# A two-layer Hyena and RWKV-7 step on one core: SyncE's load queue of the RWKV scan in another order

## The chip, the cores and the metric

The kernel runs on one core of one Trainium2 chip. The metric is the device time of one execution of the whole program in microseconds (us), lower is better. PE is TensorE (matmuls and transposes), DVE is VectorE, ACT is ScalarE, POOL is GpSimd, and SP is SyncE, which here does nothing but request DMA transfers in the order in which its instructions stand.

## The reference, cut to what matters

640 tokens (512 latent tokens and 128 context tokens, 1024 wide) pass a Hyena layer and then a bidirectional RWKV-7 layer with 32 heads of 64. All is float32. The change touches only the recurrence of the second layer, which is run forward and backward for each head:

```python
def _wkv7_scan(r, w, k, v, a, b, s0, reverse):
    """RWKV-7 state recurrence S_t = S_{t-1}(diag(w_t) + a_t^T b_t) + v_t^T k_t ; y_t = S_t r_t.
    r,w,k,v,a,b: (B, T, H, N) float32; s0 (B, H, N, N) [value, key]."""
    def step(S, inp):
        r_t, w_t, k_t, v_t, a_t, b_t = inp
        sa = jnp.einsum("bhvk,bhk->bhv", S, a_t)
        S = S * w_t[:, :, None, :] + sa[..., :, None] * b_t[..., None, :] + v_t[..., :, None] * k_t[..., None, :]
        return S, jnp.einsum("bhvk,bhk->bhv", S, r_t)
...
    decay = jnp.exp(-jnp.exp(-jax.nn.softplus(-w_raw) - 0.5))
...
    o_f, s_f = _wkv7_scan(r_h, decay_h[0], k_dir[0], v_h, -kk, kk * iclr_h[0], s0_f, False)
    o_b, s_b = _wkv7_scan(r_h, decay_h[1], k_dir[1], v_h, -kk, kk * iclr_h[1], s0_b, True)
```

w (decay) and the learning rate iclr come from two small low-rank weights for each direction, kk is the key scaled and normalised by head. Returned are the outputs of both token groups and the final states of the context.

## The kernel before, in words

The program is a sequence of stages, each a block in which the five engines run their own instruction lists and meet only by semaphores: modulation vectors, filter, Hyena input, convolution, Hyena output, RWKV projections (`rwkv_in`, which leave keys and receptances in `scratch_rk_d` and values and gates in `scratch_vz_d`), the scan (`rwkv_scan`, L1358), and the output stage. The change is in the scan.

The scan takes 16 rounds, one for each pair of heads (128 of the 2048 inner channels). The 640 tokens stand as 10 chunks of 64. A round has two parts:

- a chunk part: PE forms the products of the scaled keys (`e_decays` with `e_bk`, the "scores"), turns the keys (into `BKT`) and the matrix `C_` (into `CT`), and then inverts a triangular 64x64 system for every chunk in five levels. A level is: transposes of `e_F` (T), the products Y (`M` with `CTm`), which ACT copies into `BDY`, the products Z (`BDY` with `M2T`), which DVE adds into `e_F`. Between them PE fills in scores left over (L1601).
- a state part of eight steps, in which the states go through the chunks (`BDS` with `e_ar`, `BDW` with `e_Q`, `UV` with `BKT`) and the outputs are summed from `BDV`, `BDU`, `BDS`. Its last output product bears the mark "O" (L1752).

While round i runs, the engines also prepare round i+1 ("prep"), in pieces put between the main work by hand: ACT squares and scales the new keys `e_k` (`e_kk`, L1771 to L1773, behind a wait for the keys' load) between the copies of `CT` and the first copy of `BDY`; PE applies the small weights `e_w` and `e_a` in levels 4 and 5; DVE builds `e_decays`, its last product of the prep bears the mark "ar"; PE transposes the start states `st` behind "O" (mark "S0", L1570). The pieces stand in each engine's one list, so a piece that waits holds up the main work that stands behind it. ACT's copies of `BDY` stand behind `e_kk`.

SP requests the loads of a round in three groups. `load_keys(j)` (L1459): keys `e_k` (128x640), the small weights `e_w` and `e_a`, receptances `e_r`, and the two start states, six transfers, behind a wait for "S0" of round j-1. `load_values(j)` (L1471): 14 transfers of the values into `BDV` and `UV`; PE waits for them at L1706, where the state part begins. `copy_ar(j)` (L1483): a copy of `e_decays` into `e_ar`, 1280 KB inside the on-chip memory, behind a wait for "ar" of round j; PE waits for it at L1707. `BDV`, `UV` and `e_ar` have one buffer each, which round i reads until its "O". POOL builds the masks `CTm`, and stores states and outputs (`Osb`) of a round behind its end; it goes on to the next round only when those stores have landed (L1524).

`Steps.now(label, i)` is the semaphore value at which the step with that label is done in round i; `Steps.before(label, i)` is the value at which it was done in round i-1 (for round 0 it holds from the start). `rounds` runs the first 15 rounds in a loop with `has_prep` true, the 16th behind it with `has_prep` false; PE's list is unrolled.

Of the kernel before, what the change touches and what calls it, by code (L numbers as in the profile page):

```python
# [1357 lines left out]
def rwkv_scan(nc, A, G, M):  # L1358
# [37 lines left out]
    with ExitStack() as st:  # L1396
# [29 lines left out]
        main, prep = kinds("main", ("pe", "act", "dve", "pool")), kinds("prep", ("pe", "act", "dve"))  # L1426
# [8 lines left out]
        def rounds(eng, kind, body):  # L1435
            steps = [s[kind] for s in (main, prep) if kind in s]
            with eng.Fori(0, KE - 1) as i:
                for s in steps:
                    s.n = 0
                body(i, True)  # L1440
            for s in steps:
                s.n = 0
            body(KE - 1, False)
# [10 lines left out]
        with nc.Block() as block:  # L1454
            @block.sync
            def _(sp):
                sp.wait_ge(s_z, 6)

                def load_keys(j):  # L1459
                    ch = bass.ds(j * P, P)  # L1460

                    sp.wait_ge(prep["pe"].sem, prep["pe"].before("S0", j))
                    sp.dma_start(k[:, :], A["rk_d"][1, ch, :]).then_inc(s_l["k"], 16)
                    for n, src, dst in (("w2", "rw_w2", lw2), ("a2", "rw_a2", la2)):
                        sp.dma_start(dst[:, :], A[src][0].rearrange("z r e -> (z r) e")[:, ch]).then_inc(s_l[n], 16)
                    sp.dma_start(r[:, :], A["rk_d"][0, ch, :]).then_inc(s_l["r"], 16)
                    for d, n in enumerate(("state_rwkv_fwd", "state_rwkv_bwd")):
                        src = A[n][0, 0].rearrange("h v k -> v h k")[:, bass.ds(2 * j, 2), :]
                        sp.dma_start(st0[HALVES[d], :].rearrange("v (h k) -> v h k", h=2), src).then_inc(s_l["st"], 16)

                def load_values(j):  # L1471
                    v_t = A["vz_d"][0].rearrange("(c t) n -> t c n", t=C)
                    for h in range(2):
                        sp.dma_start(BDV[HALVES[h], :, HALVES[h]], v_t[:, :, bass.ds(j * P + 64 * h, 64)]).then_inc(s_l["v"], 16)
                    ch = bass.ds(j * P, P)
                    sp.dma_start(UV[HIGH, 0:NS:3, :], v_t[:, 0:CS, ch]).then_inc(s_l["v"], 16)
                    sp.dma_start(UV[HIGH, 5:9:3, :], v_t[:, CS:NC, ch]).then_inc(s_l["v"], 16)
                    for n in range(CS):
                        sp.dma_start(UV[HIGH, 3 * n + 1, :], A["vz_d"][0, (CS - 1 - n) * C:(CS - n) * C, ch]).then_inc(s_l["v"], 16)
                    for n, c in ((3, NC - 1), (4, NC - 2)):  # L1480
                        sp.dma_start(UV[HIGH, 3 * n + 2, :], A["vz_d"][0, c * C:(c + 1) * C, ch]).then_inc(s_l["v"], 16)

                def copy_ar(j):  # L1483
                    sp.wait_ge(prep["dve"].sem, prep["dve"].now("ar", j))
                    sp.dma_start(ar[:, :, :, :], decays[:, :, :, :]).then_inc(s_ar, 16)

                def body(i, has_prep):
                    if has_prep:
                        load_keys(i + 1)
                        sp.wait_ge(main["pe"].sem, main["pe"].now("O", i))  # L1490
                        load_values(i + 1)
                        copy_ar(i + 1)
                load_keys(0)
                load_values(0)
                copy_ar(0)
                rounds(sp, "pe", body)

            @block.gpsimd
# [32 lines left out]
            def _(pe):  # L1531
# [41 lines left out]
                def body(i, has_prep):  # L1573
# [117 lines left out]
                    def o_terms(now, most):  # L1691
                        while terms and terms[0][0] <= now and most:
                            _, c, a, b = terms.pop(0)
                            at_ = left.pop(0)
                            out = ps[HALVES[c % 2], c // 8, c % 8 // 2 * P:(c % 8 // 2 + 1) * P]
                            last = mm(out, a, b, at_ not in opened, at_ not in left)
                            opened.add(at_)
                            most -= 1
                        if not terms:
                            return last  # L1700
# [440 lines left out]
```

## Time and profile before

| | |
|---|---|
| runs shown: median of 2 | 3990.89 us (3990.87 to 3990.91) |
| the profiled execution, its own time | 3992.75 us |
| span of the profiled execution, first to last instruction | 3990.7 us |
| busy: PE / PE weight loads / DVE / ACT / POOL | 85% / 52% / 43% / 23% / 6% of the span |
| mean granted TensorE clock | 0.911 |
| DMA, mean | 69 GB/s |
| the scan's rounds 1 to 14, as SP's value requests stand (2318.55 to 3701.08 us) | 1382.5 us |

The page gives busy shares over the whole span; the stages have different limits, so the scan is read by its own stretch. In the rows further down, a time at a row's start is us from the start of the span. In a timeline the second number is the us that the row covers, `x20` the number of instructions in it, and the bracket at the end the idle time of that engine just before, with what ended it. A `PEclk` of 1.00 is TensorE's full clock (2.4 GHz), 0.50 half of it (1.2 GHz). `L104`, `L115` and `L118` are helpers, so tile names tell the place.

### The profile page before, as it was taken

The page shows a single profiled execution, that of the slowest core. Times are in us where ns is not written, and L with a number is a line of the kernel's source. Part 1 is how long each engine was busy: PE and PEld are TensorE (multiplying, and loading weights), DVE is VectorE, ACT ScalarE, POOL GpSimd, SP SyncE. Part 2 cuts the span into 40 slices and gives each one's busy share as a digit, 9 for nine tenths or more (in the row PEclk, how much of TensorE's full clock was granted, in tenths as well). Part 3 has the DMA queues.
Part 4 walks back from the last instruction along what each step waited for, and adds up shares of the span by engine and source line. Part 5 has one row for each costly group of instructions (what it writes and reads, how often), then busy time and mean ns, then how long its engine had stood idle before and what let it go on. Part 6 is the DMA issues. An engine that isn't in the chain of part 4 may idle for free. (4 is left out here: it accounts for less than half of the span.)

```text
span 3990.7 us, 50708 instructions
## 1 busy us (share of the span) xinstructions
PE 3373.1 (85%) x18946; PEld 2066.4 (52%) x18946; DVE 1728.8 (43%) x3104; ACT 914.6 (23%) x1968; POOL 257.2 (6%) x346
## 2 busy tenths in 40 slices
PE   7599999898898685999997788888887888888759
PEld 1255555434434342555443566666666666666624
DVE  0222222266676413100001655555555555555467
ACT  0222222100000011000000333433333433333311
POOL 0000000000000000000001011111111111111100
PEclk9799999798898897999999788998889899998979
DMA  6222222311120230323221111111111111111162
GB/s 251 69 89 88 88 84 84 117 32 48 37 71 26 85 123 22 98 89 125 80 103 61 33 37 36 37 36 37 36 37 36 37 36 37 36 36 37 32 242 85
DMA packets 223386, 276.66 MB, mean 69 GB/s; under 512 B 41412, under 2 KB 168916, under 8 KB 218757
## 3 DMA queue, kind: packets, MB, share of 16 engines
q1 hardware_dynamic: 208760, 223.59, 17.8%
q0 software_dynamic: 14480, 50.87, 3.3%
q8 instruction: 124, 2.03, 0.2%
q14 instruction: 22, 0.17, 0.0%
HBM read 199.94 MB, written 53.49 MB: 64 GB/s over the span
## 5 line engine op out<-in xcount | busy, mean ns | idle before, releaser
L104 PE MATMUL ps<-hT,hw 128*128 128x512 f32 (+1 forms) x2048 | 562.2, 435 | 6.5 <-DMA hw<-in_hy_w_in 6.5
L104 PEld LDWEIGHTS ps<-hT,hw 128*128 128x128 f32 x2048 | 313.0, 192 | 253.1 <-issue 253.1
L104 PE MATMUL ps<-mix,rw 128*128 128x512 f32 (+1 forms) x1024 | 283.1, 440 | 10.9 <-DMA rw<-in_rw_w_k 5.7
L104 PE MATMUL ps<-rwv,mix 128*128 128x512 f32 x640 | 274.9, 592 | 0.8 <-ACT rout L118 0.8
L104 PE MATMUL ps<-BDS,e_ar 128*64 128x128 f32 x1152 | 176.2, 293 | 80.5 <-DVE BDS L115 40.4
L104 PEld LDWEIGHTS ps<-mix,rw 128*128 128x128 f32 x1024 | 157.3, 194 | 136.7 <-issue 136.7
L104 PEld LDWEIGHTS ps<-rwv,mix 128*128 128x128 f32 x640 | 121.5, 190 | 153.6 <-issue 152.6
L118 ACT ACTIVATE BDY<-ps 64x384 f32<-64x384 f32 (+1 forms) x320 | 138.2, 432 | 269.9 <-PE ps L104 263.6
L104 PE MATMUL ps<-BDV,AK 128*64 128x128 f32 x1280 | 184.8, 307 | 0.0
L104 PE MATMUL ps<-e_decays,e_bk 64*64 64x128 f32 x2560 | 184.4, 295 | 0.0
L104 PE MATMUL ps<-BDY,M2T 128*64 128x128 f32 x1600 | 120.3, 303 | 73.3 <-ACT BDY L118 70.3
L115 DVE TENSOR_TENSOR BDS<-ps,e_pcd 64x128 f32<-64x128 f32 x224 | 64.6, 288 | 240.4 <-PE ps L104 236.9
L118 ACT ACT_TABLE_LOAD x70 | 89.8, 1283 | 344.4 <-PE ps L104 237.1
L104 PEld LDWEIGHTS ps<-e_decays,e_bk 64*64 64x64 f32 x2560 | 153.3, 145 | 23.5 <-issue 21.7
L104 PEld LDWEIGHTS ps<-BDS,e_ar 128*64 128x64 f32 x1152 | 108.2, 140 | 108.7 <-DVE BDS L115 44.9
L1514 POOL TENSOR_TENSOR CTm<-CT,tab 128x384 f32<-128x384 f32 (+1 forms) x160 | 134.6, 862 | 444.7 <-PE ps L104 285.6
L107 DVE SCALAR_TENSOR_TENSOR mix<-xx,col,hT 128x640 f32<-128x640 f32 x48 | 38.6, 879 | 287.5 <-PE ps L104 287.5
L112 DVE TENSOR_SCALAR hcv<-hpad,hpc 128x641 f32<-128x641 f32 x48 | 29.6, 616 | 306.8 <-ACT hpad L118 306.8
L118 ACT ACTIVATE osave<-ps 128x512 f32<-128x512 f32 x64 | 38.2, 597 | 534.1 <-PE ps L104 517.1
L115 DVE TENSOR_TENSOR M<-e_F,tab 64x384 f32<-64x384 f32 (+1 forms) x320 | 155.6, 486 | 9.9
L104 PE MATMUL ps<-hsd,dft 128*128 128x512 f32 x288 | 140.8, 652 | 17.0 <-DVE hsd L115 17.0
L1646 PE MATMUL ps<-tab,e_F 128*128 128x128 f32 x400 | 80.4, 316 | 88.1 <-DVE e_F L115 53.4
(229 smaller groups left out, 5140.0 us busy)
## 6 DMA issues: line engine op xcount, KB each, us to landing
hw<-in_hy_w_in SPq DMA_DIRECT2D x64, 512.0 KB, 4.1
aw<-in_ada_w SPq DMA_DIRECT2D x16, 1536.0 KB, 6.8
e_ar<-e_decays SPq DMA_DIRECT2D x16, 1280.0 KB, 6.7
scratch_vx_d<-hot POOLq DMA_DIRECT2D x32, 320.0 KB, 2.8
scratch_rk_d<-rout POOLq DMA_DIRECT2D x32, 320.0 KB, 3.5
scratch_vz_d<-rtok POOLq DMA_DIRECT2D x40, 256.0 KB, 2.3
rw<-in_rw_w_r SPq DMA_DIRECT2D x16, 512.0 KB, 4.0
rw<-in_rw_w_k SPq DMA_DIRECT2D x16, 512.0 KB, 4.0
```

Of the source, the lines that this page charges most:

```text
L104: return nc.tensor.matmul(out, lhsT, rhs, start=first, stop=last)
L107: return nc.vector.scalar_tensor_tensor(out=out, in0=in0, scalar=scalar, in1=in1, op0=op0, op1=op1)
L112: return nc.vector.tensor_scalar(out, in0, s1, s2, op0, op1)
L115: return nc.vector.tensor_tensor(out, a, b, op)
L118: return nc.scalar.activation(out, in_, f, **kw)
L1514: main["pool"].did(nc.gpsimd.tensor_tensor(CTm[:, lv % 2, cs, :], CT[:, cs, :], m, MUL), ("CTm", lv, g))
L1646: last = nc.tensor.transpose(ps[:, T_BANK[g], (p - q.start) * P:(p - q.start + 1) * P], F[:, 2 * p:2 * p + 2, :], ident)
```

## The change

The values of a round are requested in that round itself and no more in the round before: the prologue has no `load_values(0)`; each round requests first the keys, small weights and states of the next round, then its own values (behind a wait for "O" of the round before), and then waits for its own "O" and requests the copy into `e_ar` for the next round. No transfer is added, removed or resized, and the other engines' lists stay as they are.

```diff
                 def body(i, has_prep):
                     if has_prep:
                         load_keys(i + 1)
+
+                    sp.wait_ge(main["pe"].sem, main["pe"].before("O", i))
+                    load_values(i)
+                    if has_prep:
                         sp.wait_ge(main["pe"].sem, main["pe"].now("O", i))
-                        load_values(i + 1)
                         copy_ar(i + 1)
                 load_keys(0)
-                load_values(0)
                 copy_ar(0)
                 rounds(sp, "pe", body)
```

In SP's list at the start of the scan (before its loop) the rows stand as follows; `BDV` and `UV` are the values, `e_ar` the copy, `scan_prep_dve` the semaphore of DVE's preparation.

```order
 L1469 DMA st<-in_state_rwkv_fwd 64x2x64
 L1469 DMA st<-in_state_rwkv_bwd 64x2x64
-L1474 DMA BDV<-scratch_vz_d 64x10x64 x2
-L1476 DMA UV<-scratch_vz_d 64x8x128
-L1477 DMA UV<-scratch_vz_d 64x2x128
-L1479 DMA UV<-scratch_vz_d 64x128 x8
-L1481 DMA UV<-scratch_vz_d 64x128 x2
 L1485 DMA e_ar<-e_decays 128x2560 [waits scan_prep_dve]
 L1437 UNCONDITIONAL_BRANCH
```

The 14 value transfers of round 0 are gone from here, and the copy follows the states directly.

At the end of the loop's body and behind the loop; `scan_main_pe` is the semaphore of PE's main work, on which "O" is counted, and the branch closes the loop, whose first rows are the keys.

```order
 L1481 ISA
 L1481 DMA UV<-scratch_vz_d 64x128 x2
-L1484 ISA
+L1494 REGISTER_ALU
+L1484 ISA [waits scan_main_pe]
 L1485 DMA e_ar<-e_decays 128x2560 [waits scan_prep_dve]
 L1437 REGISTER_ALU
 L1437 COMPARE_AND_BRANCH
+L1474 DMA BDV<-scratch_vz_d 64x10x64 [waits scan_main_pe]
+L1474 DMA BDV<-scratch_vz_d 64x10x64
+L1476 DMA UV<-scratch_vz_d 64x8x128
```

The wait for "O" of the present round has moved from ahead of the values to between the values and the copy, so that only the copy and, over the branch, the next keys stand right behind it; the values of the last round now stand behind the loop.

## Rows read from the trace of the kernel before

**Rows 1.** Stretches: us, busy PE, PEld, DVE, ACT, POOL, clock, DMA; rounds 1, 3.
```profile
2318.55:2417.55 99.00, 81.92 (x798) 65.54 (x798) 58.38 (x123) 39.05 (x92) 10.61 (x13) 0.90 0.13 37
...
2516.62:2613.52 96.90, 78.38 (x798) 62.53 (x798) 58.38 (x123) 39.06 (x92) 10.59 (x13) 0.93 0.14 38
```

**Rows 2.** Waits of rounds 1 to 14: us in total, times, longest.
```profile
ACT e_kk L118 <- DMA e_k<-scratch_rk_d: 102.8, 14, 8.8
...
PE ps L104 <- ACT BDY L118: 68.8, 14, 7.3
```

**Rows 3.** Timeline of PE and ACT over round 1.
```profile
2318.44 0.33 PE L1570 MATMUL ps<-tab,st 128*128 128x128 f32 x1
2325.90 1.31 PE L104 MATMUL ps<-tab,C_ 128*64 128x128 f32 x20 [0.20 <-ACT BKT L118]
2331.23 2.40 PE L104 MATMUL ps<-M,CTm 128*64 128x128 f32 x20
2336.42 1.55 ACT L118 ACTIVATE e_kk<-e_k,e_pc 128x640 f32<-128x640 f32 x2 [7.04 <-DMA e_k<-scratch_rk_d]
2339.13 2.40 PE L104 MATMUL ps<-BDY,M2T 128*64 128x128 f32 x20 [4.17 <-ACT BDY L118]
2371.06 0.65 PE L104 MATMUL ps<-BDV,AK 128*64 128x128 f32 x4
2417.44 0.33 PE L1570 MATMUL ps<-tab,st 128*128 128x128 f32 x1
```

**Rows 4.** Timeline of SP's queue at the start of round 1, and of round 15.
```profile
2318.55 1.39 SPq L1474 DMA_DIRECT2D BDV<-scratch_vz_d  x2
...
2326.86 1.77 SPq L1481 DMA_DIRECT2D UV<-scratch_vz_d  x2
2328.77 0.51 SPq L1485 DMA_DIRECT2D e_ar<-e_decays  x1
2329.86 0.34 SPq L1463 DMA_DIRECT2D e_k<-scratch_rk_d  x1
...
2335.06 0.61 SPq L1469 DMA_DIRECT2D st<-in_state_rwkv_bwd  x1
...
3701.08 1.39 SPq L1474 DMA_DIRECT2D BDV<-scratch_vz_d  x2
```

**Rows 5.** Timeline of SP, PE and ACT at the start of round 0.
```profile
2225.82 0.35 SPq L1463 DMA_DIRECT2D e_k<-scratch_rk_d  x1
2234.03 1.31 PE L104 MATMUL ps<-tab,C_ 128*64 128x128 f32 x20 [0.20 <-ACT BKT L118]
2238.53 1.55 ACT L118 ACTIVATE e_kk<-e_k,e_pc 128x640 f32<-128x640 f32 x2 [1.02 <-DVE e_pc L1875]
2243.03 1.31 PE L104 MATMUL ps<-BDY,M2T 128*64 128x128 f32 x20
```

**Rows 6.** Granted clock by stretch: round 1 behind the wait, round 0 at its masks.
```profile
2338.50:2341.00 2.50, 1.87 (x18) 1.90 (x20) 0.28 (x1) 1.24 (x3) 0.00 (x0) 0.50 0.00 0
...
2239.50:2242.00 2.50, 2.50 (x24) 2.04 (x22) 0.69 (x1) 1.33 (x3) 1.20 (x2) 0.50 0.03 7
2242.00:2244.50 2.50, 2.34 (x38) 1.92 (x36) 1.24 (x2) 0.97 (x3) 0.95 (x2) 0.98 0.00 0
```

**Rows 7.** From request to landing: the keys' line, then the last value transfers' line.
```profile
DMA to landing us min/median/max: 3.1/6.5/8.2
...
DMA to landing us min/median/max: 2.0/2.1/2.7
```

**Rows 8.** POOL's output store of round 0 (in round 1): its issue, its landing, POOL's next work.
```profile
2320.58 0.90 POOL L1521 DMA_DIRECT2D scratch_o_d<-Osb  x1
...
scratch_o_d<-Osb POOLq DMA_DIRECT2D x1, 320.0 KB, 4.5
...
2328.28 0.99 POOL L1514 TENSOR_TENSOR CTm<-CT,tab 128x384 f32<-128x384 f32 x1 [6.80 <-ACT CT L118]
```

**Rows 9.** Timeline of PE at the first level of round 15.
```profile
3717.42 1.31 PE L104 MATMUL ps<-BDY,M2T 128*64 128x128 f32 x20
```

## The prediction

> **What bounds the kernel now.** I first took the busy shares by stretch, since the change is in the scan alone. Rounds 1 to 14 of the scan are nearly alike: 99.00 us for the first of them, 96.90 for the quickest, round 3, both with the same count of instructions and at a mean clock of 0.90 and 0.93 [rows 1]. From the first value request of round 1 (2318.55) to that of round 15 (3701.08) [rows 4] it is 1382.5 us, or 98.75 us a round. PE is busy some 82 us of it, but that includes matmuls at half clock, so the share alone says little.
>
> Then I read the list of waits over those 14 rounds. ACT waits in each round for the DMA of the next round's keys, 102.8 us in 14 times; PE waits in each round for ACT's copies of `BDY`, 68.8 us in 14 times [rows 2]. The two belong together, as the timeline of round 1 shows: ACT sits 7.04 us before `e_kk`, which needs the keys, then does it in 1.55, and only then copies `BDY`; PE sits 4.17 us for that copy before the level's products Z [rows 3]. So one load that serves only the next round stops the present round's chain.
>
> Why the keys are late is in SP's queue. "O" of a round ends just before SP goes on (PE's next product, the transpose of the states, starts at 2318.44 [rows 3]). SP then requests 14 value transfers from 2318.55 to 2328.63, the copy at 2328.77, and only at 2329.86 the keys [rows 4], which ACT has in use at 2336.42. A request to landing takes 6.5 us in the median and 8.2 at most [rows 7]. The values, for which the keys queue, are first read at 2371.06, where the state part starts [rows 3].
>
> **Where the trace already shows the new order.** In round 0 the queue had requested its values long before, in the prologue, so the copy and the keys came first at the round's start, the keys at 2225.82. There ACT waits 1.02 us for a column that DVE copies (`e_pc`) and not for the keys, and PE starts the products Z with no idle time at 2243.03, 9.00 us behind the products of `C_` (2234.03) [rows 5]. In round 1 the same distance is 2325.90 to 2339.13, 13.23 us [rows 3]. Round 15, which prepares no further round and so waits for no keys, starts Z without idle time too [rows 9]. These two rounds are the measure for the sum.
>
> **The change part by part.**
>
> *Keys earlier.* Behind "O" now stands the copy, then the keys. The copy is requested at about 2318.7 where 2328.77 was; the keys follow it by the same 1.09 us (2329.86 less 2328.77), so at about 2319.8. Their own wait, for the transpose of the states, is over at 2318.44 + 0.33 = 2318.77 [rows 3], ahead of that. They land at 2319.8 + 6.5 = 2326.3, or 2328.0 with the longest landing. ACT can't use them before the column `e_pc` is there: in round 0 that let `e_kk` start 4.50 us behind the products of `C_` (2238.53 less 2234.03 [rows 5]), which is 2330.4 in round 1, so 2.4 us are spare even then. The wait for keys goes, and what is late next is what round 0 shows: 1 us for the column, beside PE's work.
>
> *What a round gains.* From the products of `C_` to the transpose of the states at the round's end: 2234.03 to 2318.44 = 84.41 us in round 0, 2325.90 to 2417.44 = 91.54 in round 1 [rows 3, 5]. The difference is 7.13 us. It is the wait of 4.17 and 2.96 more, which is clock: behind the wait the clock is at 0.50 and the 20 products Z take 2.40 us; in round 0 it was at 0.50 before them too but is back at 0.98 when they run, in 1.31 [rows 3, 5, 6].
>
> The Trainium skill ("TensorE: Matmul & The Clock Gate", section on how the oscillation bites in real kernels) describes a loop whose wait for a DMA sends the clock down, so that each piece behind it begins cold. The trace agrees for the stretch behind this wait, but it also shows the clock down at 2239.50 of round 0 where no DMA was waited for, so not every low stretch of the round is the stall's; by the rule the clock's 2.96 us come back with the wait, and if the clock fell all the same only the wait would.
>
> *Sum.* By the pair of rounds 14 x 7.13 = 99.8 us. By the mean: a new round takes 7.35 (2318.55 to 2325.90) + 84.41 + 0.11 = 91.87, the old mean is 98.75, so 14 x 6.88 = 96.3. I take 98. Rounds 0 and 15 gain nothing, they never had the wait. The profiled execution takes 3992.75, less 98 is 3894.75; the runs shown lie 1.86 below it, so 3893. That is 2.5%; about 2% (80 us, 5.7 a round) is what a measurement of this kernel tells from no change.
>
> *Values later.* They now follow the keys: the six requests of that group take 2329.86 to 2335.67 = 5.8 us [rows 4], so values are requested from about 2325.6 to 2335.7 and the last lands by 2338.4 (2.7 at most [rows 7]). They are needed at 2371.06 less the 7 us won, 2364. Some 25 us cover them; I cost them at nothing, and without that cover each us late would cost 14. In round 0 they leave the prologue, where only the copy stood behind them, and that waits for DVE's whole preparation of round 0 ("ar") in any case; the keys at 2225.82 [rows 5] stay where they are: nothing.
>
> *Copy earlier, waits and register work on SP.* The copy is read at the state part as the values are, earlier is no gain. Behind SP's new wait for "O" stand the copy and the next keys, neither of which may start sooner. One register instruction and one wait more are tens of ns in the 1.09 us already counted.
>
> *New company.* The copy now runs while PE forms the scores and DVE their masks, and beside POOL's store. In round 0 it ran beside the same scores, and the idle time before the products of `C_` is 0.20 us there as in round 1, where it did not [rows 3, 5], so nothing for that. POOL's store is not in round 0. It is requested at 2320.58, lands 4.5 us later, and POOL goes on at 2328.28, when ACT's `CT` lets it [rows 8]: 3.2 us of cover on POOL. Bounds: nothing (as with the values beside it now), or what its landing grows beyond that; below nothing it can't go, since nobody waits for it now. I take nothing.
>
> The Trainium skill ("DMA: Bandwidth & Descriptors", section on queues, rings and completion order) says that a DMA engine takes turns between the queues for which it has work. It speaks against the change: the store and the copy slow each other, and the keys queue behind the copy. No run here shows the pair; by the rule the keys would lose a part of their 2.4 us of cover and the sum would stand.
>
> **The rivals.**
>
> *Only the wait goes.* The clock falls later in the level loop just as it does now behind the wait, so the 2.96 us stay: gain 68.8 [rows 2], time 3990.89 - 68.8 = 3922. For it: the clock is low in each round at other places too, mean 0.90. Against it: rounds 0 and 15 had no wait and ran the products Z at full clock. 0.07.
>
> *More of the low clock goes.* Round 3 is 2.10 us shorter than round 1 with 3.5 us less of PE busy time and clock 0.93 [rows 1]; if all rounds fall so, 14 x 2.1 = 29 more, 3864. 0.05.
>
> *No gain.* The keys, requested earlier, still land only when the values are through, or another input of `e_kk` takes their place. It would stay at 3991. Against it: round 0, where keys behind a copy were there in time. 0.04.
>
> *Slower.* The mechanism is POOL's store. POOL stands at L1524 until it has landed, its masks `CTm` come behind, and PE's products Y behind these. The copy now moves beside it. Past 3.2 us of delay POOL itself is late; the first mask is ready at 2328.28 + 0.99 = 2329.27 [rows 8] and PE begins the products Y at 2331.23 [rows 3], 2.0 us later, so beyond 5.2 us each us costs 14. It turns slower when the delay passes 5.2 + 7.1 = 12.3 us, a landing of 16.8 instead of 4.5; with 22.5 (18 us of delay) it is 14 x (18 - 12.3) = 80 us slower, 4071. Nothing in the trace comes near such a landing. 0.03.
>
> **How the numbers follow.** The forecast, full gain with a clock as in round 0, 0.81, at 3893. The range runs from more clock (3864) to the wait alone (3922). Faster by over 2% (below 3911): forecast and more clock, 0.81 + 0.05, less 0.01 for a forecast that falls short by 18 us, 0.85. Within 2%: the wait alone, no gain and that 0.01, 0.12. Slower by over 2%: 0.03.
>
> **What would show it.** In the changed kernel's profile SP should request the keys about 1.1 us behind the copy and the copy right behind "O"; ACT's wait for the keys' DMA should be gone from rounds 1 to 14, PE's wait for `BDY` at the first level with it; the distance from the products of `C_` to Z should be about 9.0 us with Z in 1.31; a round should be near 92 us. The first state products should show no wait for the values' DMA. I am wrong if ACT still waits for keys, if Z still runs in 2.40 (then 3922), if a wait for `BDV` or `UV` shows at the state part, or if POOL's masks are late behind the store.

## The result, and the profile after

The changed kernel takes 3875.22 us (median of 2 runs, 3871.68 and 3878.77) against 3990.89: the ratio is 0.971, 95% interval 0.9668 to 0.9752. It is faster by 2.9%, inside the stated range (3864 to 3922) and 18 us below the stated 3893. In the three later sets of runs the kernel before lay between 3977.7 and 3997.7 in single runs, with medians of 3984.8 to 3988.0, so some us of the 116 may belong to the first set; two variants below that win the same wait stand 110 and 111 us under the kernel before beside them.

SP's queue at the start of round 1 of the changed kernel (as [rows 4]): the copy stands right behind "O", the keys 1.08 us behind it, the values last.

```profile
2310.57 0.50 SPq L1485 DMA_DIRECT2D e_ar<-e_decays  x1
2311.65 0.34 SPq L1463 DMA_DIRECT2D e_k<-scratch_rk_d  x1
2312.18 1.51 SPq L1465 DMA_DIRECT2D e_w<-in_rw_w  x1
...
2317.92 0.61 SPq L1469 DMA_DIRECT2D st<-in_state_rwkv_bwd  x1
2318.83 2.04 SPq L1474 DMA_DIRECT2D BDV<-scratch_vz_d  x2
...
2327.79 1.11 SPq L1481 DMA_DIRECT2D UV<-scratch_vz_d  x2
```

PE, ACT and POOL in the same round (as [rows 3], [rows 5]):

```profile
2317.83 1.31 PE L104 MATMUL ps<-tab,C_ 128*64 128x128 f32 x20 [0.20 <-ACT BKT L118]
2320.25 3.50 POOL L1516 TENSOR_TENSOR CTm<-CT,tab 128x384 f32<-128x384 f32 x4 [6.84 <-ACT CT L118]
2322.32 1.55 ACT L118 ACTIVATE e_kk<-e_k,e_pc 128x640 f32<-128x640 f32 x2 [1.01 <-DVE e_pc L1877]
2323.27 2.40 PE L104 MATMUL ps<-M,CTm 128*64 128x128 f32 x20
2326.83 1.31 PE L104 MATMUL ps<-BDY,M2T 128*64 128x128 f32 x20
2355.85 0.65 PE L104 MATMUL ps<-BDV,AK 128*64 128x128 f32 x4
2402.29 0.33 PE L1572 MATMUL ps<-tab,st 128*128 128x128 f32 x1
```

ACT now waits 1.01 us for the column and not for the keys. The products Z stand 9.00 us behind the products of `C_` (2317.83 to 2326.83) with no idle time, at full clock, and the round's end 84.46 us behind them. In this round POOL still waits for ACT's `CT`, not for its store, which landed 7.0 us after its request; in other rounds the store is later (see the account of the prediction).

The waits over rounds 1 to 14 (as [rows 2]) have no row of keys any more, and 0.3 us is left of PE's wait for `BDY`:

```profile
ACT e_kk L118 <- DVE e_pc L1877: 17.6, 14, 1.6
...
PE ps L104 <- ACT BDY L118: 0.3, 1, 0.3
```

The stretches of rounds 1, 2 and of all of rounds 1 to 14 (columns as in [rows 1]):

```profile
2310.57:2402.49 91.92, 78.28 (x798) 62.61 (x797) 58.27 (x123) 38.99 (x93) 10.59 (x13) 0.94 0.14 40
2402.49:2491.84 89.35, 75.62 (x798) 60.41 (x797) 58.72 (x123) 39.00 (x93) 10.51 (x13) 0.98 0.15 41
...
2310.57:3583.50 1272.93, 1082.00 (x11159) 866.37 (x11158) 818.05 (x1722) 545.90 (x1289) 147.75 (x182) 0.96 0.14 40
```

and the same 14 rounds of the kernel before, with the wait of PE that grew, from both kernels (before first):

```profile
2318.55:3701.08 1382.53, 1132.82 (x11159) 906.81 (x11159) 816.92 (x1722) 546.69 (x1288) 148.30 (x182) 0.91 0.13 37
...
PE ps L1646 <- DVE e_F L115: 44.6, 70, 1.1
```
```profile
PE ps L1648 <- DVE e_F L115: 54.3, 83, 1.1
```

So the 14 rounds went from 1382.5 to 1272.9 us, 109.6 less. The books close: PE's wait for `BDY` fell by 68.5; PE's busy time, for the same 11159 matmuls, by 50.8, since more of them run at full clock (0.91 to 0.96); and 9.7 came back as PE's wait for DVE's `e_F` (83 times where it was 70, with DVE's busy time the same to 1.1 us): 68.5 + 50.8 - 9.7 = 109.6.

### The profile page after: what moved, and what is told of

It is laid out like the page before. It is cut to its first block and busy times, and to the rows that moved or that the text cites. A ratio compares the mean times of both kernels' runs of the same rounds, so it can differ in the third digit from the quotient of the medians.

```text
span 3870.0 us, 50738 instructions
## 1 busy us (share of the span) xinstructions
PE 3316.6 (86%) x18946; PEld 2022.4 (52%) x18946; DVE 1729.9 (45%) x3104; ACT 913.4 (24%) x1968; POOL 256.3 (7%) x346
## 5 line engine op out<-in xcount | busy, mean ns | idle before, releaser
L104 PE MATMUL ps<-e_decays,e_bk 64*64 64x128 f32 x2560 | 170.5, 280 | 0.0
L1648 PE MATMUL ps<-tab,e_F 128*128 128x128 f32 x400 | 71.6, 290 | 97.9 <-DVE e_F L115 63.1
L104 PE MATMUL ps<-ow,oy 128*128 128x512 f32 x320 | 143.2, 610 | 11.8 <-DMA oy<-scratch_y_d 11.8
L104 PEld LDWEIGHTS ps<-e_decays,e_bk 64*64 64x64 f32 x2560 | 142.1, 137 | 19.7 <-issue 17.9
```

Of the source, the lines that this page charges most:

```text
L104: return nc.tensor.matmul(out, lhsT, rhs, start=first, stop=last)
L1648: last = nc.tensor.transpose(ps[:, T_BANK[g], (p - q.start) * P:(p - q.start + 1) * P], F[:, 2 * p:2 * p + 2, :], ident)
```

## The experiments

The theory is the one on record: only the lateness of `e_k` costs, through `e_kk` and `BDY`, and it brings the clock down behind it. The rivals are named with each run.

**The copy first, the keys still last.**

```diff
                         sp.wait_ge(main["pe"].sem, main["pe"].now("O", i))
-                        load_values(i + 1)
                         copy_ar(i + 1)
+                        load_values(i + 1)
```

> The order of before, but with the copy into e_ar ahead of the values: copy, values, keys. Theory (the keys' lateness is the cost): the keys are requested as late as before, some 11 us behind O, so the wait of ACT for them stays; with the copy already gone from the queue they may land up to 2 us sooner. ACT's wait in rounds 1 to 14 stays at 70 to 103 us, the time between 3955 and 3992. Rival (it was the earlier copy, or the values no longer queued ahead of it, that gained): near the changed kernel, 3875.

3987.93 us, ratio to the kernel before 1.0007 (0.9997 to 1.0016): nothing gained. The rows of this kernel: its queue in round 1, and its waits in all rounds.

```profile
2315.90 0.53 SPq L1485 DMA_DIRECT2D e_ar<-e_decays  x1
2316.53 2.45 SPq L1474 DMA_DIRECT2D BDV<-scratch_vz_d  x2
...
2330.53 0.34 SPq L1463 DMA_DIRECT2D e_k<-scratch_rk_d  x1
...
ACT e_kk L118 <- DMA e_k<-scratch_rk_d: 98.2, 14, 8.1
...
PE ps L104 <- ACT BDY L118: 60.9, 14, 5.6
```

The copy is as early as in the changed kernel and both waits stay. The earlier copy is not the cause.

**The keys first, the copy last.** Behind "O" of round i: keys of round i+2, values and copy of round i+1.

```diff
-                    if has_prep:
-                        load_keys(i + 1)
-                        sp.wait_ge(main["pe"].sem, main["pe"].now("O", i))
-                        load_values(i + 1)
-                        copy_ar(i + 1)
+                    sp.wait_ge(main["pe"].sem, main["pe"].now("O", i))
+                    if has_prep:
+                        load_keys(i + 2)
+                    load_values(i + 1)
+                    copy_ar(i + 1)
...
-                rounds(sp, "pe", body)
+                load_keys(1)
+                with sp.Fori(0, KE - 2) as i:
+                    body(i, True)
+                body(KE - 2, False)
```

> Behind O the keys of the round after next, then the next round's values, then the copy: the copy is as late as before or later, by the six key requests (6 us). Theory: ACT's wait for keys is gone, the time is that of the changed kernel, 3867 to 3885. Rival (the copy's place gained): 3991, or slower, with a wait for e_ar at the state part.

3873.83 us, ratio 0.9726 (0.971 to 0.9743), as the changed kernel, though the copy is requested some 14 us later than there. Only that the keys stand ahead of the values counts.

**Of the group, `e_k` alone.** The changed kernel with the other five requests of `load_keys` in a function of their own, behind the values.

```diff
                     load_values(i)
                     if has_prep:
+                        load_rest(i + 1)
```

> The changed kernel, but only e_k goes ahead of the values; small weights, receptances and states stand behind them. Theory: only e_k is waited for at the round's start, the rest is needed at level 4 (some 34 us behind O) or later, so 3867 to 3885. Rival (the whole group has to be early): a wait for e_w or e_a at level 4, above 3900.

3874.69 us, ratio 0.9724 (0.9708 to 0.9741): the one transfer of the keys is the whole effect.

**Part of the values ahead again.** The changed kernel with the first 8, or the first 12, of the 14 value transfers requested for the next round ahead of the copy, the rest (`load_values_rest`, split off from `load_values`) behind the keys.

```diff
-                    sp.wait_ge(main["pe"].sem, main["pe"].before("O", i))
-                    load_values(i)
+                    load_values_rest(i)
                     if has_prep:
                         sp.wait_ge(main["pe"].sem, main["pe"].now("O", i))
+                        load_values(i + 1)
                         copy_ar(i + 1)
                 load_keys(0)
+                load_values(0)
                 copy_ar(0)
```

> The changed kernel with 8 of the 14 value transfers of the next round back ahead of the copy and the keys. The keys are then requested about 6.9 us behind O and land about 13.5 to 14 us behind it; the column e_pc is there 11.9 us behind O, and PE needs BDY so that keys up to about 13.7 us behind O cost it nothing. Theory (only what passes that point costs): ACT waits 1.5 to 2 us a round for keys, PE 0 to 0.5 for BDY, time 3868 to 3892. Rival (each value ahead of the keys costs its share): 8/14 of the gain gone, about 3938.

> The same with 12 of the 14 value transfers ahead. Keys requested about 9.5 us behind O, landing about 16 behind it: ACT waits some 4 us a round, PE about 2.3 for BDY, and where the clock falls with that wait up to 3 us more. Theory: 2.3 to 5.3 us a round lost of the gain, time 3907 to 3950. Rival (share by share): 12/14 gone, about 3969.

3889.05 us (0.9748, 0.9732 to 0.9764) with 8, and 3944.46 (0.9883, 0.9867 to 0.99) with 12. Waits of rounds 1 to 14, first with 8, then with 12 ahead:

```profile
ACT e_kk L118 <- DMA e_k<-scratch_rk_d: 44.5, 14, 4.1
...
PE ps L104 <- ACT BDY L118: 12.7, 10, 1.9
```
```profile
ACT e_kk L118 <- DMA e_k<-scratch_rk_d: 82.1, 14, 6.5
...
PE ps L104 <- ACT BDY L118: 48.0, 14, 4.5
```

Of ACT's wait, 44.5 - 12.7 = 31.8 and 82.1 - 48.0 = 34.1 us, some 2.3 a round, reach nobody: so much slack the chain has, and past it the lateness goes through to PE. With 8 ahead ACT's wait came out at 3.2 us a round where 1.5 to 2 was expected, and PE's at 0.9 where 0 to 0.5 was. The rounds 1 to 14 as a whole, with 8 and with 12 ahead:

```profile
2312.49:3599.49 1287.00, 1085.33 (x11159) 867.20 (x11159) 815.25 (x1722) 545.83 (x1288) 148.15 (x182) 0.95 0.14 40
...
2312.39:3660.44 1348.05, 1118.95 (x11159) 895.13 (x11159) 815.94 (x1722) 545.87 (x1288) 148.01 (x182) 0.92 0.14 38
```

Against the changed kernel's 1272.9, 12.7 us of wait go with 14.1 us more, 48.0 with 75.1, and the 68.8 of the kernel before with 109.6: 1.1, 1.6 and 1.6 us for each us of wait. What is more than the wait is mostly clock: PE's busy time for the same 11159 matmuls is 1082.0, 1085.3, 1119.0 and 1132.8 us in that order, the mean clock 0.96, 0.95, 0.92 and 0.91.

**The wait filled, the keys still late.** In the kernel before, PE multiplies the identity with itself where it would sit idle; nobody reads it. `warm(0, 60)` issues 60 such products (18 in the second run).

```diff
+                        if lv == 1 and has_prep:
+                            A_(("CT", 0))
+                            warm(0, 60)
                         for g, q in enumerate(PAIRS):
                             if lv == 1:
                                 A_(("CT", g))
```

> The kernel before with 60 products of the identity with itself, whose result nobody reads, ahead of the first level's products Z in rounds 0 to 14, where PE now sits idle for the late BDY. The keys stay late. Theory in two parts: the wait itself (4.9 us a round) cannot be won this way, the clock's part (3 us a round) can, since PE stays busy: Z then in 1.31 us and the time 3945 to 3965. Rival (the low clock behind the wait has nothing to do with the wait): Z still in 2.40, time 3991 or above, by what the 60 products overrun the wait.

4071.68 us (1.0223, 1.0205 to 1.0241): a miss in the size of the edit. One product is two matmul instructions, and the 60 of a round took far longer than the wait:

```profile
2339.25 13.66 PE L104 MATMUL ps<-tab 128*128 128x128 f32 x120
2352.85 1.31 PE L104 MATMUL ps<-BDY,M2T 128*64 128x128 f32 x20
```

Still, by an estimate with the mean wait of 4.91 (68.8 / 14) they add 14 x (13.66 - 4.91) + 13.66 (round 0, which has no wait) = 136 us, and the run is only 87 slower than the kernel before: 49, or 3.5 a round, came back, with Z in 1.31. With 18:

> The kernel before with 18 products of the identity, not read by anybody, where PE sits idle for the late BDY (60 took 13.66 us, so 18 take 4.1, about the wait). Theory: the wait stays, filled, and the clock's part comes back, about 3 us a round: Z in 1.31, less the 4.1 us in round 0, which has no wait: 3940 to 3965. Rival (the clock's part does not belong to the wait): 3985 or above.

3947.37 us (0.9904, 0.9887 to 0.9921), 40.6 less than the kernel before beside it, though ACT waits 103.5 us for keys as ever. The 18 products take 4.29 us, and of PE's wait 7.0 us are left, in 6 rounds. Round 0, which has no wait, is 1.7 us longer (93.66 before and 95.35 here, from the copy's request to the next values'). Rounds 1 to 14, which took 1382.53 in the kernel before:

```profile
2317.79:3656.28 1338.49, 1142.43 (x11663) 923.31 (x11663) 816.03 (x1722) 546.80 (x1288) 148.26 (x182) 0.96 0.14 38
```

So they won 44.0 us, or 3.1 each, with the wait still there and its time filled: that is the clock's part of the wait, shown by itself.

**The values as late as they can be.**

```diff
-                    sp.wait_ge(main["pe"].sem, main["pe"].before("O", i))
+                    sp.wait_ge(main["pe"].sem, main["pe"].now(("T", 5, 0), i))
                     load_values(i)
```

> The changed kernel with the values of a round requested only when PE's first transposes of level 5 are done, some 32 us later than in the changed kernel. In its trace the values have landed about 24.9 us before the state part. Theory (they have a cover of about 25 us and nothing else hangs on them): PE waits about 6.9 us for them in each of 16 rounds, time 3980 to 4035. Rival (the values' cover is smaller, as traffic or the queue makes it): more than 4035; rival (larger): no loss, 3875.

4005.2 us (1.0044, 1.003 to 1.0058). The values, 32 us later, are now waited for where the state part starts, and what follows runs at half clock (1.12 us where the changed kernel has 0.65):

```profile
2374.41 1.12 PE L104 MATMUL ps<-BDV,AK 128*64 128x128 f32 x4 [5.68 <-DMA UV<-scratch_vz_d]
...
PE ps L104 <- DMA UV<-scratch_vz_d: 77.5, 13, 6.6
```

The second line covers 13 of the rounds: 6.0 us a round where 6.9 was expected. The values are requested 40.0 us behind the copy (2363.38 and 2323.38) where the changed kernel has 8.3, so 31.7 later; less 6.0 the cover is about 26 us, and past its end each us is a wait of PE.

**A version that beats both.** The changed kernel's rounds still hold low clock at two places. The same idle products go there: 4 ahead of the first transposes (behind a wait for `Arb`), 8 in the first step of the state part.

```diff
+                    D_(("Arb", 0))
+                    warm(6, 4)
                     for lv in range(1, LEVELS):
...
                         if n in (0, 2, 5):
                             next(later, None)
+                        if n == 0 and has_prep:
+                            wait(prep["act"], ("lora", *LORAS[-1]), j)
+                            warm(6, 8)
```

> The changed kernel with 4 products of the identity, not read by anybody, in PE's idle time between the products of C_ and the first transposes (about 0.9 of 2.2 us can be filled there without holding anybody up). In 9 of 14 rounds the clock is at 0.50 for some 3.4 us from about 5 us behind the products of C_. Theory (that low stretch comes from the idle time ahead of it): it goes, and with it the about 1.2 us by which the products Y are slower, in those rounds: 3855 to 3868. Rival (the idle left is still too much, or the low stretch comes from the 64-row products): 3872 to 3885.

> The changed kernel with 8 such products where PE waits 1.9 us for the first new states (BDS) in the state part, in rounds 0 to 14. Behind that wait the clock is at 0.50 for up to 6.8 us in 9 of 14 rounds. Theory (the low stretch comes from that wait and the small products ahead of it): it goes, with 2.5 to 3 us in those rounds: 3840 to 3860. Rival (not its cause): 3872 to 3885.

> Both fills. Theory: the sum of both, rounds of about 88 us, 3820 to 3850. Rivals: as for each.

The first alone: 3869.54 us (0.9709, 0.9685 to 0.9733), between the two ranges expected; it can't be told from the changed kernel. The second alone: 3843.0 (0.9644, 0.9627 to 0.966). Both: 3825.6 (0.9599, 0.9583 to 0.9615), 4.0% below the kernel before and the best version here. Two rounds each, of the first alone and then of both:

```profile
2313.78:2403.01 89.23, 76.41 (x806) 61.32 (x805) 58.48 (x123) 38.99 (x93) 10.53 (x13) 0.98 0.15 41
2403.01:2494.62 91.61, 79.11 (x806) 63.36 (x805) 58.59 (x123) 38.99 (x93) 10.52 (x13) 0.94 0.14 40
```
```profile
2307.14:2394.79 87.65, 76.76 (x822) 61.68 (x821) 58.51 (x123) 38.98 (x93) 10.54 (x13) 1.00 0.15 42
2394.79:2482.44 87.65, 76.69 (x822) 61.69 (x821) 58.24 (x123) 38.99 (x93) 10.60 (x13) 1.00 0.15 42
```

With both, the clock stays at 1.00 through these rounds, and 12 more products make them shorter. So it is in 13 of the 14 rounds (87.6 to 87.8 us); one took 90.58 at a mean clock of 0.96. With the first alone the mean clock is that of the changed kernel's two kinds of round.

## Why the prediction was right, and where its size was off

- *The keys' request.* "At about 2319.8", 1.3 us behind "O": measured 2311.65, 1.1 us behind the point where SP goes on. It landed in 7.2 us in the median, 8.5 at most, where 6.5 and 8.2 were taken; the 2.4 us of cover held. Right; the runs with the copy first, the copy last and `e_k` alone show that this one transfer is the cause.
- *The wait and the clock.* Round 0 as the measure: 84.41 us from `C_` to the end, 84.46 measured in round 1. The wait filled with idle products shows the clock's part alone at 3.1 us a round; 2.96 was stated.
- *The sum, 98, was too small.* Of the two sums on record, the one by the mean took 91.87 us for a new round. Nine of the 14 rounds took 91.8 to 92.0, but five took 89.1 to 89.4. 14 x 91.87 = 1286.2 against 1272.9 measured: 13.3 us, which with the 96.3 make the 109.6. The term that was mis-sized is the new round, taken from a single round 0 as if every round had its low stretches. The rival that more of the low clock goes was half true; it was given 0.05 as a case for all rounds and should have been a share of the rounds.
- *The rest.* The profiled execution is 121.1 us shorter, 11.5 more than the 109.6. By the rows' times some 4.8 lie ahead of the scan, 3.2 in its prologue and round 0, 3.1 behind round 14, in work that the change doesn't touch but for the prologue. Why is open; the single runs of the kernel before differ by as much.
- *Values, copy.* Costed at nothing, with a cover of 25 us for the values: the run with late values shows 26.
- *POOL's store, the slower rival.* Its mechanism is there, its size is not: beside the copy the store lands 8.5 us after its request in the median (8.9 at most) where it took 4.8 before, 3.7 later. Costed at nothing, it does delay POOL: in the 8 of the 14 rounds in which it takes 8.5 or more, the first mask starts 3.5 to 3.9 us behind the products of `C_`, in the other 6 it starts 2.4 behind. Round 2 is one of the 8:

```profile
2409.75 1.31 PE L104 MATMUL ps<-tab,C_ 128*64 128x128 f32 x20 [0.20 <-ACT BKT L118]
2413.58 4.97 POOL L1516 TENSOR_TENSOR CTm<-CT,tab 128x384 f32<-128x384 f32 x6 [8.55 <-ACT CT L118]
2414.91 1.31 PE L104 MATMUL ps<-M,CTm 128*64 128x128 f32 x20
```

  The row names `CT`, but a store of 8.8 us lands at 2412.93, 0.65 ahead of the mask's start; it is 0.6 to 0.7 in all 8. So the sign "POOL's masks are late behind the store" came true. It costs nothing, as the delay stays within the 5.2 us that reach PE and no row of PE waits for a mask, but little was left: this mask (0.99 us, as before) is done at 2414.57, 0.3 ahead of the products Y.
- *Only the wait goes, no gain.* Fallen: PE's busy time fell by 50.8 us, and the keys were in time.

## What to carry to other kernels

In a list of requests that is worked off in order, the request to put first is the one that is read first, not the one whose buffer comes free first: here 14 transfers with 25 us of slack stood ahead of one with none. A round of the same kernel that lacks the wait (here the first and the last) is a good measure of what its removal brings, clock and all; but one round is one sample of the clock. And where PE waits a microsecond or two at a fixed place, a few products that nobody reads can be worth more than they cost; which places pay has to be measured, as here one alone brought nothing that can be told, the other 32 us, and both together 50.

## What was not expected of the hardware

- The requests themselves take longer behind the copy: in the changed kernel `e_w` and `e_a` hold SP 1.66 and 1.55 us in the median of rounds 1 to 14 (1.2 at least) with the 1280 KB copy just ahead, and 0.33 and 0.38 in the run with the copy last, whose queue in round 1 is this:

```profile
2312.72 0.34 SPq L1463 DMA_DIRECT2D e_k<-scratch_rk_d  x1
2313.26 0.34 SPq L1465 DMA_DIRECT2D e_w<-in_rw_w  x1
2313.70 0.38 SPq L1465 DMA_DIRECT2D e_a<-in_rw_a  x1
```

- A transfer's landing hangs on what stands just ahead of it: the keys' 320 KB land in 2.9 us (median) behind the values with the copy ahead of these, in 3.1 with nothing just ahead, and in 6.5 to 7.2 right behind the copy.
- Filling one of two idle places doesn't free the clock of the other: in the run with the first fill alone the low stretch left the place behind `C_`, and in rounds of 91.61 us the clock was low in the later levels and in the state part instead (0.66 from 2441 to 2446 us, 0.50 from 2456 to 2461). Why it falls there in some rounds and not in others is open. The late store of POOL doesn't sort them: in the run with the copy last POOL never idles longer ahead of a mask than in the kernel before (7.1 us at most for `CT`), and its rounds are of the same two kinds, 89.1 and 91.9 us.
